# Feed-forward upward products as one 512-column and one 256-column matmul, with DVE adding the two halves

## The reference

```
D_MODEL = 1024
SEQ = 256
D_FF = 2816

def causal_dwconv(x, w):
    """Causal depthwise conv over positions. x: (B, S, C), w: (K, C); y[t] = sum_k w[k] x[t-K+1+k]."""
    ...

def conv_glu_ffn(xn, w_up, conv_w, w_down):
    u = causal_dwconv(xn @ w_up, conv_w)
    g, val = jnp.split(u, 2, axis=-1)
    return (jax.nn.silu(g) * val) @ w_down

def first_block(...):
    for l in range(DEPTH):
        ...
        x = x + conv_glu_ffn(rms_norm(x, ffn_norm[l]), ffn_w_up[l], ffn_conv_w[l], ffn_w_down[l])
    return x
```

## Time and profile before

| | us |
|---|---|
| median of three executions (1785.67 to 1792.23) | 1790.43 |
| the profiled execution, own time | 1794.11 |
| its span (first to last instruction) | 1792.3 |
| PE busy (its share in the chain of work that ended last: 87%) | 1722.5 |
| DVE busy | 860.0 |
| ACT busy | 488.2 |

### The profile page before, as it was taken

One profiled execution on the slowest core, in us unless ns is written; L12 is line 12 of the kernel. 1 busy time (PEld: TensorE's weight loads), 2 busy tenths in 40 slices (PEclk: granted clock), 3 DMA queues, 4 the chain that ended last, 5 costly groups with the idle time before them and its releaser, 6 DMA issues.

```text
span 1792.3 us, 23432 instructions
## 1 busy us (share of the span) xinstructions
PE 1722.5 (96%) x9572; PEld 1133.6 (63%) x9572; DVE 860.0 (48%) x1512; ACT 488.2 (27%) x750; POOL 20.8 (1%) x31
## 2 busy tenths in 40 slices
PE   7998999999998999899999999989989999999997
PEld 6878999897788999744444444337674444444443
DVE  4667777674667777623233233232552332332323
ACT  4445444444445444310000000012431100010001
POOL 0100000000000000000000000000000000000000
PEclk9999999999999999999999999999989999999999
DMA  9524566565544556889999999996369999999995
GB/s 372 181 82 157 185 211 199 170 191 185 194 131 163 177 186 225 325 330 417 425 425 423 428 426 425 425 413 229 137 260 375 420 423 425 425 425 427 426 424 240
DMA packets 116617, 542.39 MB, mean 303 GB/s; under 512 B 5672, under 2 KB 51888, under 8 KB 88496
## 3 DMA queue, kind: packets, MB, share of 16 engines
q1 hardware_dynamic: 116096, 539.75, 76.4%
q10 hardware_dynamic: 432, 1.39, 0.2%
HBM read 540.07 MB, written 1.05 MB: 302 GB/s over the span
## 4 chain that ended last, share of the span: by engine, by line
PE 87%; DMA 4%; DVE 3%; ACT 2%; SPq 2%; issue 1%; POOL 0%; DVEq 0%; ACTq 0%; POOLq 0%
PE PS L1928 22%; PE PS L669 12%; PE PS L670 12%; PE PS L671 12%; PE PS L1958 11%; PE PS L1882 6%; DMA work<-w_up 4%; PE PS L516 2%; PE PS L1910 2%; SPq L2042 2%; PE PS L1911 1%; PE PS L1942 1%; ACT hs L415 1%; PE PS L1725 1%; PE PS L1426 0%
## 5 line engine op out<-in xcount | busy, mean ns | idle before, releaser
L1928 PE MATMUL PS<-ring,work 128*64 128x512 f32 x1152 | 279.3, 593 | 0.0
L2017 DVE SCALAR_TENSOR_TENSOR work<-PS,small,work 128x512 f32<-128x512 f32 x32 | 24.0, 751 | 404.5 <-PE PS L1928 404.5
L1928 PE MATMUL PS<-work 128*64 128x512 f32 x656 | 205.3, 595 | 0.0
L1928 PEld LDWEIGHTS PS<-ring,work 128*64 128x64 f32 x1152 | 91.1, 137 | 163.6 <-issue 163.4
L1958 PE MATMUL PS<-ring,work 128*64 128x512 f32 x576 | 160.2, 598 | 1.6 <-ACT work L1983 1.6
L1882 PEld LDWEIGHTS PS<-work,hs 128*128 128x128 f32 x1024 | 118.2, 194 | 27.5 <-issue 24.3
L1882 PE MATMUL PS<-work,hs 128*128 128x128 f32 x1024 | 124.3, 281 | 2.7 <-DVE work L1865 2.7
L1928 PEld LDWEIGHTS PS<-work 128*64 128x64 f32 x656 | 66.7, 138 | 92.0 <-issue 92.0
L1958 PE MATMUL PS<-work 128*64 128x512 f32 x368 | 124.3, 598 | 0.0
L1983 ACT ACTIVATE work<-PS 128x512 f32<-128x512 f32 x32 | 19.1, 598 | 334.5 <-PE PS L1942 334.5
L1143 DVE TENSOR_TENSOR r_w_lo<-ring,r_w_hi 128x1024 fp32r<-128x1024 f32 x64 | 78.2, 1225 | 66.0 <-ACT r_w_hi L1136 64.8
(11 more groups left out here) (344 smaller groups left out, 3422.1 us busy)
## 6 DMA issues: line engine op xcount, KB each, us to landing
ring<-w_gate SPq DMA_DIRECT2D x32, 2048.0 KB, 26.3
ring<-w_down SPq DMA_DIRECT2D x32, 2048.0 KB, 24.5
ring<-w_up SPq DMA_DIRECT2D x28, 2048.0 KB, 23.5
ring<-ffn_w_up SPq DMA_DIRECT2D x22, 2048.0 KB, 8.7
work<-w_gate SPq DMA_DIRECT2D x16, 2048.0 KB, 28.3
work<-w_down SPq DMA_DIRECT2D x14, 2048.0 KB, 20.3
work<-w_up SPq DMA_DIRECT2D x14, 2048.0 KB, 20.8
ring<-ffn_w_down SPq DMA_DIRECT2D x22, 1024.0 KB, 6.0
```

Of the source, the lines that this page charges most:

```text
L1928: last = nc.tensor.matmul(PS[CAP * e:CAP * (e + 1), what, :], xg[:, c, CAP * e:CAP * (e + 1)], chunk_of(w[e], c), start=(c == 0), stop=(c ...
```

## The change

The two activation parts are laid so that one access pattern takes both (`f_both`: rest first, rounded second). The weight's hi part then meets both at once, in one matmul of 512 columns that fills the whole bank: the left 256 columns get hi·rest, the right 256 hi·rounded. The weight's lo part still meets the rounded activations alone, with 256 columns, added to the right half. So a chunk has two matmuls with two weight loads, where it had three and three.

The bank now holds the output in two halves. ACT copies the left half to SBUF (`f_rest`, in the norm's tile `hs`), and DVE adds the right half to it into `f_sum` (also in `hs`). ACT's newest tap and DVE's two other taps then read `f_sum` and no longer the bank. PE waits for the four additions (`ffn_s`) before it uses the banks again, no longer for the four convolutions. ACT doesn't wait for the copy of the tap weights by itself any more (`ffn_cw` is gone).

```diff
+        f_both = placed("f_x_both", [P, 2 * n_rows], late_at, F32R)[:, :].rearrange("p (a b) -> p a b", b=n_rows)
+        f_x = [f_both[:, i, 0:DC * S].rearrange("p (c s) -> p c s", s=S) for i in (1, 0)]
+        f_rest = hs[:, 0, :].rearrange("p (a b) -> p a b", b=S)
+        f_sum = hs[:, 1, :].rearrange("p (a b) -> p a b", b=S)
...
-                            pe.wait_ge(E("ffn_u"), 4 * (s0 + s))
+                            pe.wait_ge(E("ffn_s"), 4 * (s0 + s))
...
-                            last = three_products(bank(4 + m)[:, 0:S], [v[:, c, j * P:(j + 1) * P] for v in w],
-                                                  [v[:, c, :] for v in f_x], c == 0, c == DC - 1)
+                            hi, lo = (v[:, c, j * P:(j + 1) * P] for v in w)
+                            nc.tensor.matmul(bank(4 + m, 2, S), hi, f_both[:, :, c * S:(c + 1) * S], start=(c == 0), stop=False, skip_group_check=True)
+                            last = nc.tensor.matmul(bank(4 + m)[:, S:], lo, f_x[0][:, c, :], start=False, stop=(c == DC - 1),
+                                                    skip_group_check=True)
...
             def newest(s, m):
-                act.wait_ge(E("ffn_cw"), s0 + s + 1)
                 act.wait_ge(E("ffn_u_ps"), 4 * (s0 + s) + m + 1)
+                nc.scalar.activation(f_rest[:, m, :], bank(4 + m)[:, 0:S], ACT.Copy).then_inc(E("ffn_t"), 1)
                 act.wait_ge(E("ffn_h"), 1 + s0 + s)
-                nc.scalar.activation(f_u[:, m, :], bank(4 + m)[:, 0:S], ACT.Copy,
+                act.wait_ge(E("ffn_s"), 4 * (s0 + s) + m + 1)
+                nc.scalar.activation(f_u[:, m, :], f_sum[:, m, :], ACT.Copy,
                                      scale=f_cw[:, 3 * m + 2:3 * m + 3]).then_inc(E("ffn_t"), 1)
...
             def conv(s, m):
-                dve.wait_ge(E("ffn_t"), 4 * (s0 + s) + m + 1)
-                u = bank(4 + m)
+                dve.wait_ge(E("ffn_t"), 8 * (s0 + s) + 2 * m + 2)
+                u = f_sum[:, m, :]
...
-                dve.sem_inc(E("ffn_cw"), 1)
                 for kind in (GATE, VALUE):
+                    for j in range(2):
+                        m = 2 * kind + j
+                        dve.wait_ge(E("ffn_t"), 8 * (s0 + s) + 2 * m + 1)
+                        nc.vector.tensor_tensor(f_sum[:, m, :], bank(4 + m)[:, S:], f_rest[:, m, :], ALU.add).then_inc(E("ffn_s"), 1)
                     for j in range(2):
                         conv(s, 2 * kind + j)
```

More of the change, by code:

```diff
@@ L256, in build @@
         f_h_last = [placed(f"f_h_last_{part}", [P, 2, S], f_at + 4 * (HALF * 2 + j * 2 * S), F32R) for j, part in enumerate(("hi", "lo"))]
-        f_x = [placed("f_x_hi", [P, DC, S], xnT_at, F32R), placed("f_x_lo", [P, DC, S], late_at, F32R)]
+        f_both = placed("f_x_both", [P, 2 * n_rows], late_at, F32R)[:, :].rearrange("p (a b) -> p a b", b=n_rows)
+        f_x = [f_both[:, i, 0:DC * S].rearrange("p (c s) -> p c s", s=S) for i in (1, 0)]
         assert 1040 + 6 * HALF + 4 * S <= WORK and DC * S <= n_rows
+        f_rest = hs[:, 0, :].rearrange("p (a b) -> p a b", b=S)
+        f_sum = hs[:, 1, :].rearrange("p (a b) -> p a b", b=S)
         R_AT, R_HEAD = 32, 2048
```

## The result

The changed kernel takes 1826.74 us (median of 4 runs, 1825.69 to 1832.02) against 1789.21 us for the kernel before on the same chip (4 runs, 1785.67 to 1792.23). The ratio is 1.0203 with a 95% interval of 1.0185 to 1.0222: 37.5 us slower, where 27.4 were forecast. The profiled execution has a span of 1830.2 us instead of 1792.3.

A forecast was written before the change was run, and what follows sets the result against it. PE was taken as the bound, with DVE and ACT taking over after the change. Per layer 0.2 + 6.1 + 1.3 + 4.4 + 1.7 = 13.7 us, 27.4 for both, on 1790.4 gave 1818 us; range 1804 to 1838.

The forecast's parts named there:

- The bound moves from PE to the lists: In the slabs, DVE and ACT's instruction lists would become the bound: 17.4 us a slab against PE's 16.5.
- The signs named in advance: In the profile: PE waits near 1 us at nearly every up, DVE idle twice a slab about 0.9 us.
- The rival that the lists keep up: In the slabs, DVE and ACT stay under PE's 16.5 us, so PE's whole gain comes in: 1784.7 us, 6%.
- the lap: DVE's time from one tap copy to the next, once per slab: 13.98 us without PE's waits, forecast to become 17.43.
- The gate half: Part of a slab from the tap copy's start to the rest of the gate weights: 3.10 to 4.30 us, +1.20.
- the value half: Part of a slab from the gate rest's end to the value rest's start: 1.74 to 3.99 us, +2.25.
- The range: Whole kernel, 1804 to 1838 us: free handoffs, faster taps, no clock loss below; handoffs of 0.10, down(10) at low clock above.
- PE's 5.7 us: In the ups, two matmuls a chunk instead of three save 0.008 us each, 5.7 us over 22 slabs.
- the rival "faster": The slabs stay bound by PE because DVE and ACT keep up; its whole saving comes in: 1784.7 us, chance 6%.
- The loop turns and the end: Loop turns at slabs 4, 7 and 1 add 1.3 us a layer; PE's 4.5 us wait ahead of down(10), 4.4.
- The clock: In down(10), the wait ahead may drop PE to 1.2 GHz: 1.7 us a layer taken, between 0 and 5.1.
- The rival in which the clock falls in every slab: Gaps of 1 us ahead of the ups halve PE's rate for 4 us of each slab: 1840 us, 8%.

The follow-up runs named there:

- old release: The changed kernel, but PE again waits for the four convolutions of the slab before, not the four additions: 1829.56 us, ratio 1.0219.

## Why the prediction was right, and where its sizes were off

**The bound moves from PE to the lists: right.** The lap became longer than PE's slab, and PE waits for the addition at every up. It was shown from both sides: the order alone removes all of the loss, and the matmuls' shape alone neither makes nor heals it. The signs named in advance were there: two gaps of 0.91 us in each slab between additions, and 37.2 us of additions on DVE and 31.8 of copies on ACT (37 and 33 forecast). The rival that the lists keep up is wrong for this kernel, but it describes the reordered one.

**The term that was most off is the lap**, forecast at 17.43 and measured at 17.86. Over 18 laps that is 7.7 of the 10 us missing. The other misses partly cancel, and that is luck: +1.4 in the rest of the nine laps, mostly loop turns, +1.0 ahead of up(1), +1.6 ahead of down(10), +1.9 by the clock in it, and -3.2 between the stages. The lap's own miss came in small pieces. The gate half took 4.51 us instead of 4.30, the value half 4.11 instead of 3.99, and the product waits 0.31 for the value rest instead of 0.22. Three of my inputs were too low: the handoff from DVE to ACT (0.10, four times a lap, taken as 0.04 from a single row), the wait behind the tap copy (0.14 instead of 0.06), and the tap from SBUF (0.51 instead of 0.49). The range had a handoff of 0.10 as its upper case for all eight in a lap; it was true for the four from DVE to ACT. (Its lower case counts 1.7 us for the taps, but four taps of 0.016 us in 20 laps are 1.3.) On the tap: it went from 474 ns out of PSUM to 510 out of SBUF. The Trainium skill, page "VectorE: DVE Perf Modes", section on the TRN2 errata, gives ScalarE 52 cycles more from SBUF than from PSUM, which at the 1.2 GHz of that table is an estimate of 43 ns. The trace agrees roughly, with 36. For the convolutions on VectorE the same table has 62 cycles less from SBUF than from PSUM, and there the trace doesn't agree: 479 ns before, 476 after.

**PE's 5.7 us: wrong.** The step "It becomes one of 512 and one of 256, 0.2275 + 0.1178" took the pitch of down's matmuls for the new one. I had read the difference between 2 x 0.1178 and 0.2275 as a cost per matmul, which a wider one would save. It isn't: the new 512 runs at 235 ns, twice 117.8. In this program fp32r matmuls ran at 0.443 or 0.460 ns per column, for 256 columns as for 512. Down is at the first, the steady ups of the kernel before and of the changed one at the second, whichever width they have. It made no difference to the forecast, since PE wasn't to be the bound, but the rival "faster" would have come out as no change: the reordered kernel is that case, at a ratio of 1.0002 and not at the 1784.7 us given for it.

**The loop turns and the end: right in kind.** The gap ahead of the tap copy at the turns (slabs 4 and 7) is 0.90 and 0.94 us in layer 1 and 0.73 in layer 2 (forecast 0.80), and at slab 1 it is 0.81 and 0.45 (forecast 0.46). They lie on the path. The wait ahead of down(10) is 4.8 us (forecast 4.5), 5.0 in layer 2.

**The clock: right in kind, low in size.** The gaps of about 1 us cost none: 1.00 in the slab. The long wait did, 2.8 us in layer 1 and 2.4 in layer 2, where I took 1.7 of a possible 5.1. About 13 of the 24 matmuls of down(10) ran at the 1.2 GHz level. The rival in which the clock falls in every slab is excluded for this kernel, whose gaps at the ups reached 1.8 us and once 2.6. With the old matmul widths it did fall in three of the ups, so the margin was not large, and the one row of 1.74 us in the prediction could not have shown that.

**Not foreseen:** the 3.2 us that came back between the stages, by a granted clock of 1.00 where the kernel before had 0.7. And in layer 2 the way from up(0) to up(1) grew by 1.1 us, with a wait ahead of up(1) of 2.58 us instead of 1.74.

## What to carry to other kernels

When a change adds a round trip between two engines that work through lists in order, write down the chain with its handoffs and compare that lap, not the busy time, with the bound engine's. Then look whether the order of one list can take the trips side by side: here both copies ahead of both taps took 1.86 us off a lap, and the change from 2% slower to no change. A lap must be under the bound engine's by enough to make up for the start, too, and merging instructions can lengthen it, since the first part then waits for the last. The cost per matmul should be read from two widths in the same place of the program, not from two places.

## What the runs showed of the hardware that was not expected

- Fp32r matmuls ran at two pitches at a granted clock of 1.00, 0.443 and 0.460 ns per column (113.3 and 117.8 ns for 256 columns, 226.7 and 235.5 for 512). In pairs of 512 and 256 columns, all run at the higher one; in groups of eight they averaged 0.234 and 0.115 us, between the two. With the old widths and the new copies, most ups behind a wait of PE ran at the lower one and all three without a wait at the higher one. In the kernel before, layer 1's up(0) was at the lower pitch in one profile and at the higher one in another. What decides between them stays open: it is not the number of runs in the moving operand, and grouping alone changed nothing for 256 columns.
- The handoff from DVE to an ACT that waits for it took 0.10 us in this loop, four times in each lap, while the earlier trace rows has one of 0.03. Behind the addition of 512 columns it took 0.03 too (183.54 + 0.69 = 184.23, and the tap starts at 184.26). ACT to DVE was 0.03 to 0.04 in both.
- Whether the clock falls in a stretch goes with the stage that lies ahead of it: 0.68 or 1.00 for the same code.
- The length of a gap alone doesn't tell whether the clock falls behind it. It fell behind waits of 4.85 us (changed kernel), 3.6 us (old release, up(1)) and three of 1.85 to 2.10 us (old widths), and it stayed at 1.00 behind waits of 3.05 us (old release, down(10) in layer 1), 2.58 us (changed kernel, up(1) in layer 2) and 1.87 us (old widths).
